# Conditioning pieces moved into the prompt attention, and the sample's selected branch cut in two halves

## The reference, cut to what matters

```
m = silu(c) @ w_ada + b_ada            # 9 rows (8 samples, 1 prompt), 1024 x 6144, split in 6
h = rms_norm(x) * (1 + sc1) + sh1      # pieces 0, 1 of m
attn = gate_c * compressed + gate_s * selected + gate_w * window
x = x + ga1 * (concat(norm(conv), norm(attn)) @ w_out)      # pieces 2 to 5 of m serve here
f = moe(rms_norm(x) * (1 + sc2) + sh2);  x = x + ga2 * f    # and here
```

## Time and profile before

| | us |
|---|---|
| median of 3 runs | 2215.51 |
| profiled execution | 2215.07 |
| its span, first to last instruction | 2213.3 |
| prompt attention, tiles 0 to 3 | 642 to 812 |
| prompt attention, tiles 4 to 7 | 812 to 1006 |
| sample attention | 1006.4 to 1206.3 |

### The profile page before, as it was taken

One profiled execution on the slowest core, in us unless ns is written; L12 is line 12 of the kernel. 1 busy time (PEld: TensorE's weight loads), 2 busy tenths in 40 slices (PEclk: granted clock), 3 DMA queues, 4 the chain that ended last, 5 costly groups with the idle time before them and its releaser, 6 DMA issues. The chain is left out here.

```text
span 2213.3 us, 27531 instructions
## 1 busy us (share of the span) xinstructions
PE 1931.5 (87%) x9878; PEld 1497.0 (68%) x9878; DVE 1278.9 (58%) x1961; ACT 1070.0 (48%) x1671; POOL 225.7 (10%) x203
## 2 busy tenths in 40 slices
PE   6899995999979888887976899589999999997756
PEld 2799785999977677772222355468888888885642
DVE  1534424544445667672102566599888888885626
ACT  5312113444436677771110211278788787874532
POOL 0100001000002334330110000001000000000011
PEclk9999997999976799998988999699999999998877
DMA  8321127534037210015881722289999999987636
GB/s 288 78 96 44 48 79 264 217 150 160 8 80 217 63 25 5 6 45 136 244 201 43 285 100 95 105 329 413 425 421 413 415 414 414 412 343 284 248 129 264
DMA packets 155490, 443.05 MB, mean 200 GB/s; under 512 B 37384, under 2 KB 82380, under 8 KB 123712
## 3 DMA queue, kind: packets, MB, share of 16 engines
q1 hardware_dynamic: 136272, 340.82, 41.6%
q0 software_dynamic: 13792, 81.90, 10.8%
q10 hardware_dynamic: 5328, 19.02, 2.1%
HBM read 387.21 MB, written 58.70 MB: 201 GB/s over the span
## 5 line engine op out<-in xcount | busy, mean ns | idle before, releaser
L2782 DVE TENSOR_TENSOR moe_lo<-wts_raw,moe_hi 128x2048 fp32r<-128x2048 f32 x216 | 484.8, 2288 | 115.8 <-ACT moe_hi L2679 115.7
L2679 ACT ACTIVATE moe_hi<-wts_raw 128x2048 fp32r<-128x2048 f32 x216 | 402.7, 1915 | 93.8 <-DMA wts_raw<-in_w_gate 42.7
L949 DVE TENSOR_TENSOR cmp_xl<-cmp_bank,cmp_xh 128x512 fp32r<-128x512 f32 (+1 forms) x136 | 82.6, 668 | 121.0 <-ACT cmp_xh L903 121.0
L873 PE MATMUL cmp_hp<-cmp_xh,cmp_wh 128*128 128x256 f32 (+2 forms) x512 | 150.6, 294 | 0.0
L1375 POOL TENSOR_SCALAR att_prow<-att_prow,att_scale 128x640 f32<-128x640 f32 (+15 forms) x96 | 113.4, 1194 | 342.5 <-DVE att_scale L1499 342.5
L1472 DVE TENSOR_TENSOR att_pl<-att_pT,att_ph 128x512 fp32r<-128x512 f32 (+5 forms) x148 | 101.2, 688 | 79.7 <-ACT att_ph L1403 79.4
L873 PE MATMUL cmp_hp<-cmp_xh,cmp_wl 128*128 128x256 f32 (+2 forms) x512 | 146.6, 286 | 0.0
L873 PE MATMUL cmp_hp<-cmp_xl,cmp_wh 128*128 128x256 f32 (+2 forms) x512 | 146.4, 286 | 0.0
L2550 PE MATMUL moe_G<-moe_hi,moe_xh 128*128 128x512 f32 x288 | 118.1, 410 | 24.8 <-issue 21.7
L1984 POOL DMA_INDIRECT rou_xg<-s_h,rou_idx x36 | 51.2, 1422 | 826.2 <-PE moe_XT L2569 506.7
L2590 PE MATMUL moe_Y<-moe_hi,moe_hh 128*128 128x512 f32 x288 | 115.2, 400 | 19.0 <-issue 11.1
(11 more groups left out here) (455 smaller groups left out, 4391.1 us busy)
## 6 DMA issues: line engine op xcount, KB each, us to landing
wts_raw<-in_w_gate SPq DMA_DIRECT2D x72, 1024.0 KB, 7.0
wts_raw<-in_w_up SPq DMA_DIRECT2D x72, 1024.0 KB, 7.6
wts_raw<-in_w_down SPq DMA_DIRECT2D x72, 1024.0 KB
s_yb<-moe_y ACTq DMA_DIRECT2D x36, 512.0 KB, 7.7
fro_wraw<-in_w_ada SPq DMA_DIRECT2D x4, 2048.0 KB
s_yb<-att_zero SPq DMA_DIRECT2D x1, 8192.0 KB, 32.8
one_buf<-in_w_ada SPq DMA_DIRECT2D x4, 2048.0 KB
smp_wa<-in_w_ada SPq DMA_DIRECT2D x4, 2048.0 KB
```

Source lines behind the costliest of these rows:

```text
L873: last = pe.matmul(hp[u % 2][:, 0:n], lhs[:, w, :], rhs[:, u % 3, at], start=(r == 0 and t == 0 and m == 0), stop=(r == 1 and t == 7 and m ...
L2679: act.activation(hi[p][half][:, :], raw[p][half][:, :], ACT.Copy).then_inc(hi_ready[p], 1)
L2782: dve.tensor_tensor(lo[p][half][:, :], raw[p][half][:, :], hi[p][half][:, :], ALU.subtract).then_inc(lo_ready[p], 1)
```

## The change

`order` of the prompt attention gets new items: `bias` once, `("cond", m, 0)` ahead of the first SEL tile of pair m and `("cond", m, 1)` ahead of the `back` of pair m, for m = 0 to 7 (tiles 0 to 3), and `mods` after pair 8's `back`. A `cond` item is half a piece: 2 x 8 f32 matmuls, now with a 128x128 block of `w_ada` as weights and the 9 conditioning vectors as the moving side. Results lie transposed (columns of `m` on partitions), get their bias on DVE, are turned once in `mods` and stored by eight transfers. The pieces are loaded into the sample's `kvs` buffers, two at a time; the loads of the sample's inputs and the zeroing of `s_yb` move from tile 1 to tiles 5 and 4. `ck` and `cv` are loaded behind tile 6 into the buffer that piece 0 had used.

In the sample's stage all conditioning is gone. The scores of pairs 0 to 7 go to the banks `SS`, those of pairs 8 to 15 to `SC` and `SW`; maximum, exponentials, transposes, products and sums are done by halves of 32 rows and 8 pairs. The first half's maximum stands behind pair 8 on DVE, its exponentials behind pair 9 on ACT, its transposes and products behind the scores of pairs 9 and 10 on PE.

```diff
@@ stage_prompt_attention: the order
+    put(("bias",))
...
             while backs:
-                order.append(("back", backs.pop(0)))
+                pair = backs.pop(0)
+                if pair < NM:
+                    put(("cond", pair, 1))
+                order.append(("back", pair))
+                if pair == NM:
+                    put(("mods",))
+            if k == 0 and groups[units[y][0]][1] == SEL and units[y][0] // 3 < NM:
+                put(("cond", units[y][0] // 3, 0))
@@ SP
+            sp.dma_start(brow[:, :], a["b_ada"][:, ADA1 * 512:ADA * 512].rearrange("o (r c) -> (o r) c", c=P)).then_inc(brow_in, 16)
+            sp.dma_start(cT[:, :, :].rearrange("p k n -> p (k n)"), a["s_cT"]).then_inc(cT_in, 16)
+            def load_piece(m):
+                if m >= 2:
+                    sp.wait_ge(ring_full, ring_at[("cond", m - 2, 1)] + 1)
+                n = slice((ADA1 + m) * 512, (ADA1 + m + 1) * 512)
+                sp.dma_start(wa[m % 2], a["w_ada"][0, :, n].rearrange("(k p) n -> p k n", p=P)).then_inc(wa_in[m % 2], 16)
...
-            sample.load_modulation(a, sp, tile.ada)
+            sample.load_compressed(a, sp, tile.buf)
@@ PE
+                elif ring[r][0] == "bias":
+                    pe.wait_ge(brow_in, 16)
+                    last = pe.transpose(dst[:, 0, 0:4 * NM], brow[:, :], ident[0:4 * NM, 0:4 * NM])
+                elif ring[r][0] == "cond":
+                    _, m, half = ring[r]
+                    pe.wait_ge(cT_in, 16)
+                    pe.wait_ge(wa_in[m % 2], 16 * (m // 2 + 1))
+                    for t in range(2):
+                        cols = slice((2 * half + t) * P, (2 * half + t + 1) * P)
+                        for k in range(KT):
+                            last = pe.matmul(dst[:, 0, 9 * t:9 * t + 9], wa[m % 2][:, k, cols], cT[:, k, :],
+                                             start=(k == 0), stop=(k == KT - 1))
@@ stage_sample_attention: PE
-            for m in range(MOD1):
-                condition(m)
...
                 if u:
-                    score_unit(NB + u - 1, SS, NS)
-                if u in mod_after:
-                    condition(MOD1 + mod_after.index(u))
-            score_unit(NB + NP_ - 1, SS, NS)
-            pe.wait_ge(v_kept, NP_)
-            values(2, S_)
+                    score_unit(NB + u - 1, sel_scores[(u - 1) // HU], NS)
+                if u == HU + 2:
+                    turn_half(0)
+                if u == HU + 3:
+                    values_half(0)
+            score_unit(NB + NP_ - 1, sel_scores[1], NS)
+            turn_half(1)
+            values_half(1)
```

More of the change, by code:

```diff
@@ L1202, in stage_prompt_attention @@
         acc = [s.sb(f"acc{i}", [P, NH, HD]) for i in range(2)]
+        wa = [sample.kvs[:, 2 * i:2 * i + 2, :].rearrange("p i c -> p (i c)").rearrange("p (k n) -> p k n", n=512)
+              for i in range(2)]
+        cT = s.sb("cT", [P, KT, 9])
+        brow = s.sb("brow", [4 * NM, P])
+        bT = s.sb("bT", [P, 4 * NM])
+        mT = s.sb("mT", [P, NM * NC9])
+        mrow = s.sb("mrow", [2 * NC9, NM // 2, P])
         S = s.ps("S", [P, NB_S * 512])
@@ L1210, in stage_prompt_attention @@
         q_in = [s.sem(f"q_in{i}") for i in range(2)]
+        cT_in = s.sem("cT_in")
+        brow_in = s.sem("brow_in")
+        wa_in = [s.sem(f"wa_in{i}") for i in range(2)]
+        mod_out = s.sem("mod_out")
         masks_ready = s.sem("masks_ready")
@@ L1292, in fill @@
                         last = pe.transpose(dst[:, t, :], q[i % 2][:, half * 4 + t, :], ident[:, :])
+                elif ring[r][0] == "bias":
[10 more added lines that the diff above has]
+                                             start=(k == 0), stop=(k == KT - 1))
+                elif ring[r][0] == "mods":
+                    pe.wait_ge(ring_free, ring_at[("cond", NM - 1, 1)] + 1)
+                    for j in range(NM // 2):
+                        last = pe.transpose(dst[0:2 * NC9, j, :], mT[:, 2 * NC9 * j:2 * NC9 * (j + 1)], ident[:, :])
                 else:
@@ L1396, in high @@
                     act.activation(qh[i % 2][:, half * 4:half * 4 + 4, :], src[:, :, :], ACT.Copy, scale=-1.0).then_inc(ring_high, 1)
+                elif ring[r][0] == "bias":
+                    act.wait_ge(ring_full, r + 1)
+                    act.activation(bT[:, 0:2 * NM], src[:, 0, 0:2 * NM], ACT.Copy).then_inc(ring_high, 1)
+                elif ring[r][0] == "cond":
+                    _, m, half = ring[r]
+                    at = m * NC9 + 18 * half
+                    act.wait_ge(ring_full, r + 1)
+                    act.activation(mT[:, at:at + 18], src[:, 0, 0:18], ACT.Copy).then_inc(ring_high, 1)
+                elif ring[r][0] == "mods":
+                    act.wait_ge(ring_full, r + 1)
+                    act.activation(mrow[:, 0:2, :], src[0:2 * NC9, 0:2, :], ACT.Copy).then_inc(ring_high, 1)
                 else:
@@ L1468, in low_part @@
                                              op0=ALU.mult, op1=ALU.subtract).then_inc(ring_free, 1)
+                elif ring[r][0] == "bias":
+                    dve.tensor_copy(bT[:, 2 * NM:4 * NM], src[:, 0, 2 * NM:4 * NM]).then_inc(ring_free, 1)
+                elif ring[r][0] == "cond":
+                    _, m, half = ring[r]
+                    at = m * NC9 + 18 * half
+                    c = 4 * m + 2 * half
+                    dve.wait_ge(ring_free, ring_at[("bias",)] + 1)
+                    piece = mT[:, at:at + 18].rearrange("p (b r) -> p b r", r=9)
+                    dve.tensor_tensor(piece, piece, bT[:, c:c + 2].rearrange("p (b o) -> p b o", o=1).to_broadcast([P, 2, 9]), ALU.add
+                                      ).then_inc(ring_free, 1)
+                elif ring[r][0] == "mods":
+                    dve.tensor_copy(mrow[:, 2:4, :], src[0:2 * NC9, 2:4, :]).then_inc(ring_free, 1)
                 else:
@@ L1714, in _ @@
             score_unit(NB - 1, [SW], NW)
[L1716 to L1727, removed]
             pe.wait_ge(spread_ready, 1)
```

159 lines of the change are left out of this document (83 added, 76 removed).

## The result

| | before | after |
|---|---|---|
| median, us | 2214.23 (2207.14 to 2220.40, 4 runs) | 2248.93 (2248.13 to 2251.27, 4 runs) |
| profiled execution, its span | 2215.07, 2213.3 | 2249.72, 2247.9 |

A forecast was written before the change was run, and what follows sets the result against it. It took PE at half clock to bound the prompt attention's slow stretches, and gathers the sample's pairs without conditioning: 2215.1 + 96 - 80 = 2231 us, own range 2223 to 2245, wide range 2190 to 2264.

The forecast's parts named there:

- The sample's stage: -80: Sample's stage: without conditioning its end moves from 1206.25 to 1124.8, with 1.4 us off for the clock.
- from there PE is faster than the gathers: Sample's pairs: once two gathers have landed, near 1044, PE needs 2.69 us a pair against 4.4 a gather.
- may fall between gathers: Sample's pairs: PE's clock might drop between gathers; 1.4 us allowed for it.
- gathers slower than alone: Rival, sample's stage: gathers take 5 us each, +10, 2241 us; chance 0.21 together with the slow clock.
- `ck` -4.7: Start of the sample's stage: `ck` lands earlier, so all up to the first gather moves 4.7 us ahead.
- Tail 16.5: Sample's stage, last score to store: working by halves cuts 26.1 us to 16.5.
- The prompt attention: +96: Prompt attention: pieces, lost clock, bias wait and small items, less hidden waits, add 96 us.
- 88.7: Prompt attention: total of the pieces' sixteen halves, at 3.4 us (full clock) or 6.8 (half); bounds 54.8 and 109.
- slowed native work, `mods` and the ring: Prompt attention: +13 for work slowed by lost clock, +3 for `mods`, the bias item and 18 more ring turns.
- some 20 us: First rival: by the skill page's load figure conditioning costs 55 us whatever the clock, making the change this much gain.
- the rival with 65 us of pieces: Rival, prompt attention: pieces run fast, second halves at full clock too, +59, 2194 us; chance 0.22.
- The clock hardly comes up: Rival, prompt attention tiles 0 to 3: conditioning 109, +133, 2268 us; chance 0.21 together with slow gathers.

The follow-up runs named there:

- e8_useful_fill: e7_dense_fill with pieces 6 and 7 computed behind the sample's pairs 0 to 7 in place of the idle products: 2177.58 us.
- e2_fill: Changed kernel plus two unused products of 128 rows by 512 columns behind each of the sample's pairs 0 to 8: 2245.62 us.
- e6_fill64: As e2_fill, against the changed kernel, but the extra products read 64 rows in place of 128: 2289.49 us, one run.
- e5_before_nopieces: Kernel before, with pieces 2 to 7 in the sample's stage cut to their bias product, loads left out: 2139.85 us, one run.
- e1_nogap: Changed kernel with DVE's key copies for pairs 0 and 1 moved ahead of the window branch's multiplication and reduction: 2245.72 us.
- e7_dense_fill: Changed kernel with the pieces' operands exchanged (256 columns moving), plus the edits of e1_nogap and e2_fill: 2183.29 us.

## Why the prediction was half right

*The sample's stage: -80, measured -59.* The step that failed is "from there PE is faster than the gathers", a mis-sized term of the sum: 2.69 us for a pair on PE. The earlier trace rows are true at full clock; without the pieces between them the pairs run at 0.50 and take 5.13. That is above the gathers' 4.4, so PE became the bound and never caught up the backlog of the first pairs, and the first half's 8.8 us of products were not hidden behind gathers, as the forecast had it, but added. The prediction saw that the clock "may fall between gathers" and put 1.4 us on it. First gather to last score came out 19.8 us over the 77.5; with the clock at 1.00 (e8_useful_fill) it takes 81.9 in place of 97.3. So 15.4 us come back although there is more to do, 2.7 of them from the wait for DVE (0.48 in place of 3.18), the rest from the clock. That the clock sets the pace is shown by e2_fill (products of 128 rows between the pairs: 4.55 us a pair, clock 0.99 to 1.00), by e6_fill64 (64 rows: 8.54 us, 0.50) and by e5_before_nopieces (pieces gone from the kernel before: 5.12 us). The sign stood in the trace of before: at 1067 us the same transposes and scores take 1.78 and 3.46 us. The rival *gathers slower than alone* is out: at full clock they ran at 224 GB/s.

The other terms of this stage: `ck` -4.7, measured -3.7, as the compressed scores took 6.66 us at a clock of 0.52 (5.63). Tail 16.5, measured 17.8: 16 records 9.24 us in place of 7.8, since the clock was down at their start; reduction 1.00 and choice 0.68, near the forecast (0.93 and 0.64).

*The prompt attention: +96, measured +94.8 in the stage.* This came out nearly right, but partly by luck, through errors that cancel. The halves took 97.7 us, not 88.7: the ten that the forecast had at half clock 6.94 to 6.98 us (6.8 forecast), the six that it had at full clock 3.7 to 5.6, not 3.4:

```profile
691.54 6.94 PE L1349 MATMUL att_pT<-att_cT,smi_kvs 128*128 128x9 f32 x32
...
799.75 3.72 PE L1349 MATMUL att_pT<-att_cT,smi_kvs 128*128 128x9 f32 x32
805.70 6.98 PE L1349 MATMUL att_pT<-att_cT,smi_kvs 128*128 128x9 f32 x32
```

The waits (PE, 642 to 902 us) answer to the earlier trace rows: those for ACT's copy at the backs and for POOL are gone, as forecast (-13.7); a piece is waited for once.

```profile
PE att_pT L1341 <- DMA att_brow<-in_b_ada: 7.3, 1, 7.3
...
PE att_pT L1349 <- DMA smi_kvs<-in_w_ada: 1.3, 1, 1.3
```

The bias costs 7.3 at the start, less the 2.1 that stood there before: +5.2 (4.6 forecast). What is left, 94.8 - 97.7 + 13.7 - 5.2 - 1.3 = +4.3 us, stands against 16 for slowed native work, `mods` and the ring: this term was too high. Outside the pieces PE is busy 145.5 us in the tiles 0 to 3 (243.12 - 97.66), as against 145.3 before: on balance this work did not slow.

The Trainium skill, "TensorE: Matmul & The Clock Gate", section "LDWEIGHTS (loading the stationary operand)", has one figure for the load of 128 columns, 107 ns, from which the prediction worked out 55 us for the pieces. They took 97.7, in most halves 0.22 us a record (6.97 / 32), so here the measurement decides, as the prediction had it. The gain of "some 20 us" that it put beside the 55 isn't their sum: 55 - 13.7 + 4.6 + 3 - 80 gives -31; the -21 belong to the rival with 65 us of pieces.

By its time the nearest rival was *gathers slower than alone* (2241), and that is an accident, since its cause is out. *The clock hardly comes up* (2268) has the right cause in the wrong stage: the prompt attention came out 1 us under its forecast, the sample's stage 21 us over.

## What to carry to other kernels

Work that is taken out of a loop may have been what kept the clock of the rest up: before a pair, a tile or a turn is priced by its row at full clock, look for the same instructions elsewhere in the trace at half clock (here 1.78 and 3.46 at 1067 us) and at what stood between the two. Where DMA would set the pace anyway, other work between the turns can cost less than nothing: here products of 512 columns over 128 rows made a pair 4.55 us long in place of 5.13. And look whether a product with few moving columns behind full weights can be turned round: here the same sums with the operands exchanged made 98 us into 74 and the work around them 28 us shorter.

## What was not expected of the hardware

TensorE without a gap in its work stayed at 0.50 for 57.3 us (1142.5 to 1199.8, scores of 64 rows by 480 columns and key transposes of 120 rows by 120 columns), and in e6_fill64 for over 73 us (window 1146.44 to 1220.00: PE busy 73.56 of 73.56 us at 0.50). In e2_fill, where the only difference to e6_fill64 is 128 rows in place of 64 in four records a pair, it was at 0.99 from 1149.86 to 1192.67. Weights of 9 columns did it too: the piece at 1072.20 in the kernel before brought the clock back, and in e8_useful_fill such products held it. Why the rows matter, no run here tells. What takes the clock down is not settled either: it fell behind gaps of 3.18 us (the changed kernel), 1.43 (e1_nogap) and 0.61 (e7_dense_fill), and held behind one of 1.26 between products of 128 rows (e7_dense_fill) and one of 0.45 (e8_useful_fill); in the prompt attention it fell without such a gap behind the first halves of the pieces (3.72 us ahead, 6.98 behind it, at 799.75 and 805.70).
